# A two-layer hybrid transformer backbone on one core: the weights of three groups split ahead of need, and the first modulation loaded and computed in two halves

## What is computed

```python
def rmsnorm(x, g):
    return x * rsqrt(mean(x * x, axis=-1) + EPS) * g

for l in range(2):
    last = l == 1
    sh1x, sc1x, ga1x, sh2x, sc2x, ga2x = split(silu(c) @ w_mod[l] + b_mod[l], 6)
    sh1c, sc1c, ga1c, sh2c, sc2c, ga2c = split(silu(c_ctx) @ w_mod[l] + b_mod[l], 6)
    ux = rmsnorm(h, g_pre_mix[l]) * (1 + sc1x) + sh1x
    uc = rmsnorm(hc, g_pre_mix[l]) * (1 + sc1c) + sh1c
    yx, yc = token_mixers(ux, uc, ...)       # begins with ux @ w_in[l] and uc @ w_in[l], ends with @ w_out[l]
    h = h + ga1x * rmsnorm(yx, g_post_mix[l])
    ux = rmsnorm(h, g_pre_ffn[l]) * (1 + sc2x) + sh2x
    h = h + ga2x * rmsnorm(swiglu(ux, w_ffn_in[l], w_ffn_out[l]), g_post_ffn[l])
    if not last:
        ...                                  # the same for hc
return h
```

## Time and profile before

| | |
|---|---|
| runs | 1861.15, 1853.61 and 1860.78 us, median 1860.78 |
| profiled execution, its own time | 1853.27 us |
| its span, first to last instruction | 1851.3 us |
| TensorE's mean granted clock | 0.983 of full speed (2.4 GHz) |
| busy share: TensorE, VectorE, ScalarE, GpSimd | 95%, 62%, 47%, 32% |
| moved by DMA | 224 MB, 121 GB/s on the mean |

### The profile page before, as it was taken

The page is one execution under the profiler, slowest core; times in us unless marked ns, Lnnn a source line. Parts: engine busy times, 40 slices in busy tenths (PEclk is TensorE's granted clock), DMA queues, the critical chain, the costliest instruction groups (busy, mean ns, idle before and its releaser), DMA issues. The chain is left out here.

```text
span 1851.3 us, 30506 instructions
## 1 busy us (share of the span) xinstructions
PE 1756.7 (95%) x10166; PEld 1489.5 (80%) x10166; DVE 1152.2 (62%) x2348; ACT 875.3 (47%) x1906; POOL 585.9 (32%) x555
## 2 busy tenths in 40 slices
PE   7999999999999999899999999888999999999998
PEld 3777888778788787788888888777898788979997
DVE  4256578687676765567777663555564456765655
ACT  5566555444344443552222222666565455565543
POOL 0344434455455452111111000224335654321100
PEclk8999999999999999999999999999999999999999
DMA  7222233344433325245556663233343333446665
GB/s 299 58 66 66 69 92 90 91 123 124 110 94 96 80 63 166 90 120 148 148 150 209 219 202 69 71 90 88 88 124 98 92 76 85 121 148 176 183 200 159
DMA packets 341253, 224.14 MB, mean 121 GB/s; under 512 B 57654, under 2 KB 322156, under 8 KB 340076
## 3 DMA queue, kind: packets, MB, share of 16 engines
q1 hardware_dynamic: 331692, 215.88, 41.2%
q10 hardware_dynamic: 9408, 6.32, 1.3%
HBM read 221.06 MB, written 1.07 MB: 120 GB/s over the span
## 5 line engine op out<-in xcount | busy, mean ns | idle before, releaser
L1996 PE MATMUL bank<-Uhi,w_ring 128*128 128x512 f32 (+1 forms) x1536 | 547.4, 356 | 19.0 <-ACT H L1673 7.5
L1998 PE MATMUL bank<-Uhi,w_ring 128*128 128x512 f32 (+1 forms) x1536 | 531.5, 346 | 0.0
L1997 PE MATMUL bank<-Ulo,w_ring 128*128 128x512 f32 (+1 forms) x1536 | 531.3, 346 | 0.0
L1538 ACT ACTIVATE w_ring<-load_ring 128x512 fp32r<-128x512 f32 (+3 forms) x632 | 369.8, 607 | 148.3 <-PE bank L1998 105.1
L1738 DVE TENSOR_TENSOR w_ring<-load_ring,w_ring 128x512 fp32r<-128x512 f32 (+1 forms) x424 | 319.1, 768 | 179.1 <-ACT w_ring L1538 154.9
L1996 PEld LDWEIGHTS bank<-Uhi,w_ring 128*128 128x128 f32 x1536 | 294.3, 192 | 60.3 <-ACT H L1673 10.5
L1493 POOL TENSOR_TENSOR w_ring<-load_ring,w_ring 128x512 fp32r<-128x512 f32 (+3 forms) x208 | 246.4, 1190 | 251.7 <-ACT w_ring L1538 136.2
L1998 PEld LDWEIGHTS bank<-Uhi,w_ring 128*128 128x128 f32 x1536 | 294.2, 192 | 36.4
L1997 PEld LDWEIGHTS bank<-Ulo,w_ring 128*128 128x128 f32 x1536 | 294.9, 192 | 30.1
L1481 POOL TENSOR_TENSOR Y<-Y,small 128x512 f32<-128x512 f32 x160 | 173.3, 1083 | 289.8 <-DVE small L1942 276.9
L1947 DVE TENSOR_TENSOR Z<-bank,Z 128x512 fp32r<-128x512 f32 x160 | 109.7, 686 | 96.5 <-ACT Z L1659 94.1
(11 more groups left out here) (141 smaller groups left out, 2651.3 us busy)
## 6 DMA issues: line engine op xcount, KB each, us to landing
load_ring<-in_w_in SPq DMA_DIRECT2D x192, 256.0 KB, 2.9
load_ring<-in_w_ffn_in SPq DMA_DIRECT2D x160, 256.0 KB, 3.1
mod_ring<-in_w_mod SPq DMA_DIRECT2D x96, 256.0 KB, 3.3
load_ring<-in_w_ffn_out SPq DMA_DIRECT2D x88, 256.0 KB, 3.2
mod_place<-in_w_mod SPq DMA_DIRECT2D x64, 256.0 KB, 2.8
load_ring<-in_w_branch SPq DMA_DIRECT2D x64, 256.0 KB, 2.9
mod_w<-in_w_mod SPq DMA_DIRECT2D x8, 1024.0 KB, 15.8
load_ring<-in_w_in SPq DMA_DIRECT2D x64, 128.0 KB, 2.5
```

The lines of the kernel that those rows point to most:

```text
L1538: act.activation(w_ring[:, plan.slot['w', key], 0, 0:sz], load_ring[:, plan.slot['load', key], 0:sz], ACT.Copy).then_inc(sem['w_hi'], 1)
L1996: pe.matmul(dst, lhs[0], rhs[0], start=start, stop=False)
L1997: pe.matmul(dst, lhs[0], rhs[1], start=False, stop=False)
L1998: return pe.matmul(dst, lhs[1], rhs[0], start=False, stop=stop)
```

## The change

It has two parts. **Head**: the modulation's blocks are cut in two halves, h = 0 with the columns of k-tiles 0 to 3 of shift and scale, h = 1 with those of 4 to 7. SyncE loads x and ctx first, then the eight blocks of h = 0 (512 KB each), the small loads, four weight pieces, and then the eight blocks of h = 1. In each half VectorE takes 384 columns and TensorE 640. Each half has its own sums, turns and coefficients; those of h = 1 are written between the matmuls of the first group. ScalarE copies the even input tiles, VectorE the odd ones.

**Transitions**: the eight pieces of the group behind each `output` (`nxt`) no longer go through `w_ring`; their parts have places of their own in the array Z (`w_place`) and wait only for the last piece of the projection's first half (`w_free`). A new step `early` in the list says up to which piece they may be split at that place. `begin` does all eight pieces for side 0, then all eight for side 1. For the k-tiles 3 and 5 of side 0 (`SCALED_BY_DVE`) VectorE does the scaling (`apC`) and ScalarE only the high part. The three banks of the turns follow each other in a fixed order, and the steps of `hooks` are spread anew.

```diff
 # constants
+SCALED_BY_DVE = ((0, 3), (0, 5))
-MOD0_DVE = 7 * P
-MOD0_ROWS = ((5, MOD0_DVE, 512), (6, MOD0_DVE + 512, 512), (7, MOD0_DVE + 1024, 128))
+MOD0_BANKS = ((5, 6), (3, 7))
+MOD0_DVE = 3 * P
...
 # begin
-        parts = [('gmm_a', 0, kt) for kt in range(W_RING)] + [('gmm_b', 1, kt) for kt in range(W_RING)] if both else \
-            [('gmm', 0, kt) for kt in range(W_RING)]
-        parts += [('gmm', 0, kt) for kt in range(W_RING, KT)]
+        parts = [('gmm_a' if both else 'gmm', 0, kt) for kt in range(KT)] + [('gmm_b', 1, kt) for kt in range(KT * both)]
...
-        ring = ('b3', 'pv', 'b4')[p.turns % 3]
+        ring = ('b3', 'b4', 'pv')[(side * KT + kt) % 3]
...
 # the first group of layer 0
-                if kt < KT:
+                if kt < KT and kt != 4:
                     normed((nm, 0, kt), 0, 0, None, NTOK)
                 if kt:
                     p.step('apB', (nm, 0, kt - 1), side=None, cols=NTOK)
+                    first_rows(1, ((), (), range(4), range(4, KT), (), (), (), (), ())[kt])
+                    if kt == 3:
+                        p.step('mod0row', 1)
+                    if kt == 4:
+                        first_columns(1)
+                        normed((nm, 0, kt), 0, 0, None, NTOK)
                     p.step('gmm', (first, kt - 1), side=0, both=False)
...
 # output
-            passes(0, 0, W_RING)
+            if nxt:
+                p.early[nxt] = ('piece_used', (key, early - 1))
+            for kt in range(W_RING):
+                passes(0, kt, kt + 1)
+                if nxt and kt < 4:
+                    early_split(nxt, kt + 1)
             y_sum(nmo, 1, 0)
             y_scale(nmo, 0)
             h_both(nmo, 0)
+            if nxt:
+                early_split(nxt, 6)
...
-                return {'last': [lambda turn_first: turn_first()]}
+                return {'last': [lambda turn_first: turn_first()], 2: [lambda: early_split(nxt, KT)]}
...
-                    0: [lambda: h_new(nmo, 2, 0), lambda: y_sum(nmo, 1, 3), lambda: h_new(nmo, 2, 1)],
-                    1: [lambda: y_scale(nmo, 3), lambda: h_sums(nmo, 2), lambda: h_stat(nmo, 2)],
-                    2: [lambda: h_both(nmo, 3), lambda: u_next(nmo, 2)],
-                    3: [lambda: h_sums(nmo, 3), lambda: h_stat(nmo, 3)],
-                    4: [lambda: u_next(nmo, 3)]}
+                    0: [lambda: h_new(nmo, 2, 1)],
+                    1: [lambda: y_sum(nmo, 1, 3), lambda: y_scale(nmo, 3)],
+                    2: [lambda: h_sums(nmo, 2), lambda: h_stat(nmo, 2), lambda: h_both(nmo, 3), lambda: early_split(nxt, 7)],
+                    3: [lambda: u_next(nmo, 2)],
+                    4: [lambda: h_sums(nmo, 3), lambda: h_stat(nmo, 3), lambda: early_split(nxt, KT)],
+                    5: [lambda: u_next(nmo, 3)]}
...
 # the loop that puts the splits into the list
     for st in S:
-        piece = st[0] in ('mm', 'mm_a', 'gmm', 'gmm_a', 'gmm_b', 'ym', 'ym_a', 'ym_b')
-        if piece or st[0] == 'mod0row':
+        piece = st[0] in ('mm', 'mm_a', 'mm_b', 'gmm', 'gmm_a', 'gmm_b', 'ym', 'ym_a', 'ym_b')
+        if st[0] == 'early':
+            while done < len(use) and (use[done][0] != st[1] or use[done][1] < st[2]['upto']) and (
+                    use[done][0] in p.early or ringed[place[use[done]] - W_RING] in used):
+                done = split()
+            continue
...
 # where the parts go, and what they wait for
+        def w_place(key, part):
+            if key[0] in plan.early:
+                return z((2 * key[1] + part) * PIECE, PIECE)
+            return w_ring[:, plan.slot['w', key], part, :]
+
+        def w_free(eng, key):
+            if key[0] in plan.early:
+                name, k_ = plan.early[key[0]]
+                eng.wait_ge(sem[name], count[name, k_])
+                return
...
 # VectorE
+                elif kind == 'apC':
+                    _, side, kt = key
...
+                    dve.tensor_scalar(fil[:, plan.slot['fil', ('ap', key)], 0:SEQ], ut_bank(f['bank'])[:, 0:SEQ],
+                                      is_ab(f['l'], 2 * f['which'])[:, kt, side:side + 1], shift(f['l'], f['which'], kt, side),
+                                      ALU.mult, ALU.add).then_inc(sem['ap_made'], 1)
```

More of the change, by code:

```diff
@@ L353, in turn_in @@
                 side, kt = tiles[i]
-                turn(nm, side, kt, range(NTOK // P) if whole[i] else range(2 * side, 2 * side + 2))
+                turn(nm, side, kt, range(2 * side, 2 * side + 2))
         def scale(i):
@@ L358, in scale @@
                 side, kt = tiles[i]
-                turned_by(nm, side, kt)
-                normed((nm, side, kt), l, which, None if whole[i] else side, NTOK if whole[i] else SEQ,
-                       bank=('ut', nm, side, kt))
+                kind = 'apC' if both and (side, kt) in SCALED_BY_DVE else 'apA'
+                turned_by(nm, side, kt, kind)
+                normed((nm, side, kt), l, which, side, SEQ, bank=('ut', nm, side, kt), kind=kind)
         def low(i):
@@ L365, in low @@
                 side, kt = tiles[i]
-                p.step('apB', (nm, side, kt), side=side, cols=NTOK if whole[i] else SEQ)
+                p.step('apB', (nm, side, kt), side=side, cols=SEQ)
                 for make in hooks.get(i, ()):
@@ L394, in build_plan @@
         p.step('un0', tt)
[L395 to L401, removed]
+    first_rows(0, range(6))
+    turn_in(range(1))
+    first_rows(0, range(6, 7))
+    turn_in(range(1, 2))
+    first_rows(0, range(7, KT))
     p.step('mod0row', 0)
-    p.step('mod0sum', 0)
     for l in range(DEPTH):
@@ L406, in build_plan @@
         p.step('par', l)
-    p.step('mod0turn', 0)
-    p.step('modadd', (0, 0), first=0, chunks=MOD0 // P, sides=2)
-    p.step('coef', (0, 0))
+    first_columns(0)
+    turn_in(range(2, KT))
     mods = ModPlan(p)
-    mods.enter(0, ('coef', 'coef_ready', (0, 0)))
+    mods.enter(0, ('coef0', 'coef0_ready', 1))
     for l in range(DEPTH):
@@ L893, in build_plan, with output @@
         p.step('ms', (l, KT - 1), n=nq)
-        def output(nmo, l, which, w, src, nkt, need, ends=False):
+        def output(nmo, l, which, w, src, nkt, need, nxt=None, ends=False):
             nts = nq // P
@@ L1044, in build_plan, with split @@
         p.take('load', key, (p.lo[key], key))
[L1045 removed]
+        if key[0] not in p.early:
+            p.take('w', key, ('piece_used', key))
     order, done, begun, used = [], 0, set(), set()
[L1047 to L1049 removed]
+    ringed = [key for key in use if key[0] not in p.early]
+    place = {key: i for i, key in enumerate(ringed)}
+    def split():
+        order.append(('split', use[done], {'raises': (p.lo[use[done]],)}))
+        return done + 1
+    for st in S:
+        piece = st[0] in ('mm', 'mm_a', 'mm_b', 'gmm', 'gmm_a', 'gmm_b', 'ym', 'ym_a', 'ym_b')
[4 more added lines that the diff above has]
+            continue
+        if piece or st[:2] == ('mod0turn', 0):
             first = len(begun) if st[1] not in begun else len(begun) - 1
[L1051 to L1054 removed]
+            while done < min(len(use), first + (AHEAD if piece else 2)) and (
+                    done <= first or use[done][0] not in p.early and (
+                        place[use[done]] < W_RING or ringed[place[use[done]] - W_RING] in used)):
+                done = split()
             if piece:
@@ L1392, in _ @@
+            for at, (what, key) in enumerate(plan.loads):
+                if at == L_RING:
+                    first_mod(1)
+                if what == 'consts':
                     sp.dma_start(C[:, NFIRST:], consts[:, NFIRST:NKEPT]).then_inc(s_const, 16)
@@ L1587, in _ @@
                         act.wait_ge(sem['u_turned'], count['u_turned', key])
-                        sides = range(2) if f['side'] is None else (side,)
-                        parts = [(i, at, ut_bank(f['bank'])[:, at:at + SEQ]) for i, at in zip(sides, (0, SEQ))]
-                    else:
-                        act.wait_ge(sem['xin_done'], count['xin_done', kt])
+                        parts = [(side, 0, ut_bank(f['bank'])[:, 0:f['cols']])]
+                    else:
+                        done = 'xin_right' if kt % 2 else 'xin_left'
+                        act.wait_ge(sem[done], count[done, kt])
                         parts = [(i, i * SEQ, x_tile(kt)[:, i * SEQ:(i + 1) * SEQ]) for i in range(2)]
```

231 lines of the change are left out of this document (131 added, 100 removed).

## The result

The changed kernel took 1888.6 us (median of 4 runs, 1887.0 to 1893.1) against 1858.8 for the kernel before in the same comparison: ratio 1.0168, 95% interval 1.0147 to 1.0189, slower. The forecast was 1871.8 and a range up to 1883. Its profiled execution took 1889.9 us with a span of 1888.1, 36.8 more than before (1851.3).

The account below looks back on a forecast made before the run. TensorE, busy 95% of the span, was taken as the bound. Head -2.9, T1 +6.7, T2 +4.85 and T3 +2.3 sum to +11.0 us: 1864.3 on the profiled execution, 1871.8 with 7.5 added for the median; range 1850 to 1883.

Parts of the forecast that it names:

- (4): Extra splits of later groups' pieces wait for loads and hold an apply: 7.1 us in T1, 7.1 in T2, 4.7 in T3.
- T1: The transition in layer 0 from `w_out` to FFN; forecast +6.7 us in all.
- (2): Starts of the transitions: early splits delay T1's by 2.3 us; T2's chain is later than its splits, so 0.
- T2: The transition from `ffn_out` to the mixers of layer 1; forecast +4.85 us in all.
- (5): TensorE's clock after the long waits: no difference in T1 and T2, +1.1 us in T3.
- T3: The transition in layer 1 from `w_out` to FFN; forecast +2.3 us in all.
- the head: Kernel start to the first group's end: halved modulation blocks let it end at 64.1 against 67.0, -2.9 us.
- (3): A low part and two updates of H stand on VectorE ahead of apply 3: 2.0 us in T1 and T2.
- (1): Weight groups run as halves instead of whole pieces: +0.6 us in T1, +0.8 in T2.
- The 3.5 us behind T3: Gain behind T3 with loads ahead: the 1.76 us TensorE wait and 1.7 us of low clock go.
- C: Rival: GpSimd's low parts meet updates of H, +6, head's second half at low clock, +4 to +7: +22, 1883; chance 0.10.

Follow-up runs that it names:

- e1_stop: Changed kernel with the loop of early splits ending at the named group: 1867.1 us, ratio 1.0058 to the kernel before.
- e2_store: Changed kernel with only the store of layer 1's gain rows moved behind T2's group: 1881.2 us, ratio 1.0140 to the kernel before.
- e8_rows_only: Changed kernel with the gain store in the same stretch, as rows of 512 bytes: 1873.1 us, ratio 1.0088 to the kernel before.
- e13_one: Changed kernel with only the second gain row stored as rows, the first still scattered: 1880.5 us, ratio 1.0138 to the kernel before.
- e6_before_rows: The kernel before with the gain coefficients stored as rows: 1853.7 us, ratio 0.9991 to the kernel before.
- e14_t3old: Changed kernel with T3 as in the kernel before, nothing else undone: 1879.3 us, ratio 1.0123 to the kernel before.
- e11_par: e5_rows with T3 as in the kernel before, plus layer 1's parameters loaded behind the first four weight pieces: 1850.3 us, ratio 0.9972 to the kernel before.
- e4_head: Only the head of the change, with the transitions of the kernel before: 1853.2 us, ratio 0.9997 to the kernel before.
- e9_dve: e5_rows with all low parts of the early pieces on VectorE: 1852.4 us, ratio 0.9991 to the kernel before.
- e7_later: e5_rows with the first early splits behind the sums of token tiles 0 and 1: 1857.0 us, ratio 0.9996 to the kernel before.
- e5_rows: Changed kernel with early splits stopping at their group and the gain store as rows: 1854.6 us, ratio 0.9993 to the kernel before.

## Why the prediction was wrong, step by step

The direction was right, and the step on which most of the sum rested, **(4)**, held to 0.2 us: 7.1, 7.1 and 4.7 forecast, 7.23, 6.98 and 4.58 measured, with the cause shown by e1_stop. Its working held too: in T1 the start of split 7 was put at 783.5 and was 783.42. T1 as a whole came out at +6.0 against +6.7.

**The step that failed is (2), "T2's chain is later than its splits: 0".** I took the loads ahead of T2 to land as they usually do (3.1 us is the median of the earlier trace rows) and looked no further for what else moves data at that place. The trace of the kernel before had it: a load there landed after 15.1 us. Nothing waited for it then. The change puts ScalarE's early splits ahead of the sums, and what had been slack became TensorE's time: its wait there went from 2.07 to 17.13 us (e2_store, e8_rows_only, e13_one and e6_before_rows). The stage is 17.4 us longer instead of 0.9 shorter, 18.3 us of the 25.8 by which the profiled sum was missed. At T1 the same step held: the waits ahead of the first weight matmul grew from 0.65 to 1.76 + 1.47 us, 2.6 against the forecast's 2.3.

**The second is (5), the clock.** I took +1.1 us at T3; what the group's 9.7 leave beside the hold of 4.6 is 5.1. From 1684 to 1692 TensorE was granted 0.65, and after the hold, from 1697 to 1705, 0.61:

```profile
1684.00:1692.00 8.00, 7.58 (x45) 7.50 (x45) 3.33 (x6) 5.19 (x11) 1.29 (x1) 0.65 0.06 16
...
1697.00:1705.00 8.00, 7.48 (x41) 7.48 (x42) 2.08 (x6) 4.47 (x8) 0.00 (x0) 0.61 0.23 68
```

At these clocks 5.9 of the 16 us were lost. The first follows a wait of 3.48 us ahead of T3 that I had put at nothing: there, too, the splits stand ahead of the sums, and in e14_t3old, without them, there is none. The start itself was 1.7 us late. But in e14_t3old the group is 1.5 us longer than before as well, at a lower clock behind the same waits. So not all of the 5.1 us is shown to come from the early splits.

**The third is the head**: -2.9 forecast, +0.9 measured. The sums began at 23.3 in the forecast and at 24.85 in fact, since the parameters' loads landed late (the modulation's matmuls ended in time, at 22.5). The six tiles were put at 0.51 us each, the price at the full clock, 3.1 in all with 0.9 of it hidden, and took 4.5 with 0.57 granted. What lowered the clock there is open: it fell at the same place in e11_par, whose wait ahead of the sums is 0.45 us (28 to 30 us, granted 0.50). The group from its start to its end took 34.9 us against 34.0.

**Smaller terms.** (3) was 2.0 and 2.0, and measured 1.1 and 0.4 (1.99 at T1 in e1_stop). (1) and the gains in T1 and T2 held: without the holds their groups are 3.7 us shorter than before. The 3.5 us behind T3 are there, but 1.7 of them are also in e4_head and e6_before_rows, which have the old T3, so they vary from one execution to the next; 1.8 are the change's. The 7.5 us that were added for the median were wrong: over five comparisons the kernel before has medians from 1853.9 to 1858.8, close to its profiled execution. They hid a part of the miss. The 2.6 us for a load that the prediction worked out from the Trainium skill (DMA: Bandwidth & Descriptors, section "Anatomy of one DMA — SWDGE (gpsimd) path") hold there for transfers that GpSimd issues; these loads are issued by SyncE, and the row has 3.1.

Of the rivals, C had the sign and nearly the size (1883) for a reason that was mostly wrong: the collisions with GpSimd's low parts are real (1.07 us in e9_dve), but taking them away brought nothing, and the head's second half ran at the full clock (4.59 and 4.47 us for its 32 rows of matmuls, 9.1 forecast). The lock that the Trainium skill describes (SBUF — State Buffer, section "SBUF: two separate sides") fits the rows of e7_later, where the two engines lengthened each other; the prediction had told it of two inputs from SBUF alone, and those normalized rows have one (the page names a second case, VectorE's two-port modes, which no row here can tell apart).

What stays open: how the scattered store slows the loads (2005 of its packets start between 1148 and 1152 us, and loads issued from 1151.5 to 1153.5 land only at 1170.8 and later); why e11_par's median is lower while its head is not; and what makes the stretch between the head and T1 702 to 708 us long in profiles of kernels that differ there only in the waits at its end.

## What to carry to other kernels

Before an operation is moved ahead on an in-order engine, look up the longest, not the median, of the transfers that it waits for at its new place, and what else the DMA queues do there: a slow load costs nothing until something that matters stands behind its reader. A loop that fills free places ahead of time needs a bound at both ends; here it ran on into later groups, and pieces that nobody needed yet stood ahead of those that TensorE waited for. Count also what the moved work costs the start of the next stage: here two groups got 3.7 us shorter, and their late starts took most of it back. Store small vectors as rows, turned on TensorE first, if weights are streaming beside them.

## What the runs showed of the hardware

Two stores of 1024 elements of 4 bytes kept the loads of weights slow for 17 us: 208 KB took up to 19.3 us with both (16.8 in e1_stop, 15.1 in the kernel before), 10.6 with one and 3.6 with none, and the 16 DMA engines counted as 71% busy at 22 GB/s (1160 to 1164 us). By the Trainium skill (DMA: Bandwidth & Descriptors, section "Specifications") transfers below 512 B cost a read-modify-write; the trace agrees that such stores are dear (one of 4 KB landed 12.0 us after its issue in the changed kernel), shows no read-modify-write as such, and shows that most of the price falls on the loads beside them.

Two of GpSimd's low parts of 128x512 beside two of VectorE's one-input scalings took 2.99 us, and the scalings 2.89 instead of 0.88 (e7_later, e5_rows).

With no gap in TensorE's work its turns of 128x128 took 0.75 us for a tile at a granted clock of 0.57, and 0.51 before at 1.00.
